# Output projection of seven token tiles as three one-pass products of high and low parts

## The reference

```python
mixed = jnp.concatenate([o_gla, o_gdn], axis=-1).astype(h.dtype)
h = h + mixed @ w_out[i]
h = h + moe_ffn(rmsnorm(h, g_moe[i]), w_router[i], b_router[i], w_gate_up[i], b_gate_up[i],
                w_down[i], b_down[i])
```

## Time and profile before

| | |
|---|---|
| time, three runs | 2509.98 us median (2505.41 to 2510.16) |
| the profiled execution | 2505.38 us, its span 2503.6 us |
| PE busy | 2424.4 us, 97% |
| DVE, ACT busy | 1129.9 us (45%), 581.8 us (23%) |
| route stage | about 648 to 798 us of the span |
| HBM traffic | 210 GB/s over the span |

### The profile page before, as it was taken

The page is one execution under the profiler, slowest core; times in us unless marked ns, Lnnn a source line. Parts: engine busy times, 40 slices in busy tenths (PEclk is TensorE's granted clock), DMA queues, the critical chain, the costliest instruction groups (busy, mean ns, idle before and its releaser), DMA issues. The chain is left out here.

```text
span 2503.6 us, 49492 instructions
## 1 busy us (share of the span) xinstructions
PE 2424.4 (97%) x19869; PEld 2195.0 (88%) x19870; DVE 1129.9 (45%) x1888; ACT 581.8 (23%) x1239; POOL 330.0 (13%) x345
## 2 busy tenths in 40 slices
PE   8999999999898899999999999999999999999898
PEld 6787787688444899999999999999999999999776
DVE  4667618635323523333344344344443434343485
ACT  4434324653112000001110111111111111111265
POOL 0000116252001000000010010010100101010230
PEclk9999997999998999999999999999999999999899
DMA  4111211000621866777788888899898988988562
GB/s 153 43 51 51 89 55 44 26 3 24 245 71 63 277 220 235 249 253 266 272 285 299 290 292 313 311 313 325 310 323 314 320 311 315 317 316 317 194 212 76
DMA packets 113983, 528.52 MB, mean 211 GB/s; under 512 B 15044, under 2 KB 38808, under 8 KB 64696
## 3 DMA queue, kind: packets, MB, share of 16 engines
q1 hardware_dynamic: 99160, 481.16, 54.7%
q0 software_dynamic: 14688, 45.37, 5.6%
HBM read 485.84 MB, written 40.63 MB: 210 GB/s over the span
## 5 line engine op out<-in xcount | busy, mean ns | idle before, releaser
L1886 PE MATMUL ex_psum<-ex_xT,weight_ring_a 128*128 128x134 f32 (+14 forms) x7168 | 900.4, 287 | 4.8 <-DVE ex_xT L1871 4.8
L1886 PEld LDWEIGHTS ex_psum<-ex_xT,weight_ring_a 128*128 128x128 f32 x7168 | 885.9, 192 | 6.3 <-issue 5.6
L1928 PE MATMUL ex_psum<-ex_hT,weight_ring_b 128*128 128x134 f32 (+14 forms) x4096 | 506.0, 286 | 0.0
L1928 PEld LDWEIGHTS ex_psum<-ex_hT,weight_ring_b 128*128 128x128 f32 x4096 | 503.0, 191 | 0.0
L1747 POOL DMA_INDIRECT ex_rows<-xn_dram,ex_list x170 | 164.7, 969 | 1368.2 <-DVE ex_list L1790 1317.4
L1896 DVE TENSOR_SCALAR ex_gate<-ex_psum,bias_gate_up 128x192 f32<-128x192 f32 x256 | 92.8, 404 | 526.4 <-PE ex_psum L1886 525.9
L1900 DVE TENSOR_SCALAR ex_up<-ex_psum,bias_gate_up 128x192 f32<-128x192 f32 x256 | 95.0, 413 | 379.1 <-PE ex_psum L1886 379.1
L1913 ACT ACTIVATE ex_sig<-ex_gate 128x384 f32<-128x384 f32 x128 | 66.9, 523 | 700.9 <-DVE ex_gate L1896 700.5
L1938 ACT ACTIVATE ex_yT<-ex_psum,bias_down 128x192 f32<-128x192 f32 x256 | 83.1, 436 | 564.6 <-PE ex_psum L1928 564.6
L2189 PE MATMUL project_psum<-n_hi,w_in_hi 128*128 128x512 f32 x464 | 187.0, 403 | 2.9 <-DVE n_lo L520 2.9
L2189 PE MATMUL project_psum<-n_lo,w_in_hi 128*128 128x512 f32 x464 | 181.6, 391 | 0.0
(11 more groups left out here) (347 smaller groups left out, 2475.5 us busy)
## 6 DMA issues: line engine op xcount, KB each, us to landing
weight_ring_a<-in_w_gate_up SPq DMA_DIRECT2D x224, 1024.0 KB, 5.5
weight_ring_b<-in_w_down SPq DMA_DIRECT2D x128, 1024.0 KB, 6.9
weight_ring_b<-in_w_gate_up SPq DMA_DIRECT2D x32, 1024.0 KB, 6.3
y_dram<-ex_y SPq DMA_DIRECT2D x80, 192.0 KB, 6.0
w_in_pieces<-in_w_in SPq DMA_DIRECT2D x29, 512.0 KB, 3.6
y_dram<-ex_y SPq DMA_DIRECT2D x52, 128.0 KB, 5.3
project_work<-in_x SPq DMA_DIRECT2D x8, 512.0 KB, 7.1
gates_dram<-project_work POOLq DMA_DIRECT2D x16, 256.0 KB, 2.9
```

Of the source, the lines that this page charges most:

```text
L1886: mm = pe.matmul(self.ps[:, bank, i * CAP:i * CAP + width], w[:, k, i * P:(i + 1) * P], self.xT[:, k, 0:width], start=(k == 0), stop=(k == ...
L1928: mm = pe.matmul(self.ps[:, bank, first:first + width], w[:, i, j], self.hT[:, k, 0:width], start=(k == 0 and j % 2 == 0), stop=(k == KT - ...
```

## The change

Tile 0 is projected as before. For tiles 1 to 7 the projection is done in fp32r: 48 products of 512 columns a tile (high x high, high x low, low x high for each of the 8 pieces and 2 halves).

- The high part of w_out (`w_hi`) stands in slots 3 to 6, the high part of two tiles' mixed values (`mix_hi`) in slot 2, the low part of w_out on w_out itself, and the low part of the mixed values on `g.mixA` and `g.mixB`.
- ACT makes the high parts with copies, DVE the low parts with subtractions. The low part of a piece of w_out waits for tile 0's read of that piece (`w_read`). The parts of tiles 1 and 2 are made at the start, those of tile t+3 in round t of the loops.
- PE waits for the low parts: 2t of them before tile t, and piece by piece for w_out in tile 1.
- SP issues slots 0 and 1 where all seven were, and slots 2 to 6 after the last projection, ahead of slot 7 and of the last store.
- DVE's wait for the norm's gains moves from the start of its work to in front of `norm(0)`, behind the splits.

```diff
+        slot_bytes = 4 * 2 * D
+        w_hi = standing_at("w_out_hi", [P, KT, D], g.ring_a_at + 3 * slot_bytes)
+        w_lo = standing_at("w_out_lo", [P, KT, D], g.ring_b_at + slot_bytes)
+        mix_hi = standing_at("mixed_hi", [P, 2, KT, P], g.ring_a_at + 2 * slot_bytes)
+        mix_lo = [standing_at(f"mixed_lo_{i}", [P, NH, T], at) for i, at in enumerate((g.mixA_at, g.mixB_at))]
...
-            for i in range(7):
+            def first_weights(i):
                 sp.dma_start(ring_slot(g, i).rearrange("p (k n) -> p k n", k=KT), weight_source(g, 0, i)).then_inc(g.w_in_ring[i], 16)
+
+            for i in range(2):
+                first_weights(i)
             for t in range(NT):
...
+            sp.wait_ge(proj, NT)
+            for i in range(2, 7):
+                first_weights(i)
             sp.wait_ge(squared, NT)
...
+                if t >= 1:
+                    pe.wait_ge(mix_lo_done, 2 * t)
                 for k in range(KT):
...
+                    else:
+                        if t == 1:
+                            pe.wait_ge(w_lo_done, k + 1)
+                        hi, lo = mix_hi[:, t % 2, k, :], mix_lo[k // NH][:, k % NH, t * P:(t + 1) * P]
+                        for n, (left, right) in enumerate(((hi, w_hi), (hi, w_lo), (lo, w_hi))):
+                            for half in range(2):
+                                mm = pe.matmul(ps[:, 2 * (t % 2) + half, :], left, right[:, k, half * HALF:(half + 1) * HALF],
+                                               start=(k == 0 and n == 0), stop=(k == KT - 1 and n == 2))
...
+            def split_mixed(t):
+                if t >= 3:
+                    act.wait_ge(proj, t - 1)
+                for i, of in enumerate(mixed_halves):
+                    act.copy(mix_hi[:, t % 2, NH * i:NH * (i + 1), :], of(t)).then_inc(mix_hi_done, 1)
+
+            split_mixed(1)
+            for k in range(KT):
+                if k % 2 == 0:
+                    act.wait_ge(w_out_in[k // 2], 16)
+                act.copy(w_hi[:, k, :], w_out[:, k, :]).then_inc(w_hi_done, 1)
+            split_mixed(2)
             root(0)
             root(1)
             for t in range(NT):
                 keep_turned(t)
+                if t + 3 < NT:
+                    split_mixed(t + 3)
...
-            dve.wait_ge(bc_in, 32)
...
+            split_mixed(1)
+            for k in range(KT):
+                dve.wait_ge(w_hi_done, k + 1)
+                dve.wait_ge(w_read, k + 1)
+                dve.tensor_tensor(w_lo[:, k, :], w_out[:, k, :], w_hi[:, k, :].bitcast(F32), ALU.subtract).then_inc(w_lo_done, 1)
+            split_mixed(2)
+            dve.wait_ge(bc_in, 32)
             norm(0)
...
             for t in range(NT):
+                if t + 3 < NT:
+                    split_mixed(t + 3)
                 if t + 2 < NT:
                     norm(t + 2)
```

More of the change, by code:

```diff
@@ L1385, in route, with standing_at @@
         w_out = g.ring_b[:, 1:5].rearrange("p s n -> p (s n)").rearrange("p (k n) -> p k n", k=KT)
+        def standing_at(name, shape, offset):
+            return nc.alloc_sbuf_tensor_at("rt_" + name, shape, F32R, offset=offset)
+        slot_bytes = 4 * 2 * D
[3 more added lines that the diff above has]
+        mix_lo = [standing_at(f"mixed_lo_{i}", [P, NH, T], at) for i, at in enumerate((g.mixA_at, g.mixB_at))]
         w_router = sb("w_router", [P, KT, E])
@@ L1411, in route @@
         w_out_in = [sem(f"w_out_in{i}") for i in range(KT // 2)]
+        w_hi_done, w_read, w_lo_done = sem("w_out_hi"), sem("w_out_read_by_tile_0"), sem("w_out_lo")
+        mix_hi_done, mix_lo_done = sem("mixed_hi"), sem("mixed_lo")
         w_in_s, bc_in, rows_in = sem("router_in"), sem("broadcasts_in"), sem("bias_rows_in")
@@ L1423, in route, with mixed @@
         block = ph.enter_context(nc.Block())
+        def mixed(k, t):
+            return (g.mixA if k < NH else g.mixB)[:, k % NH, t * P:(t + 1) * P]
+        mixed_halves = [lambda t: g.mixA[:, :, t * P:(t + 1) * P], lambda t: g.mixB[:, :, t * P:(t + 1) * P]]
         @block.sync
@@ L1466, in project_tile @@
                     pe.wait_ge(summed, t - 1)
+                if t >= 1:
+                    pe.wait_ge(mix_lo_done, 2 * t)
                 for k in range(KT):
[L1468 to L1474, removed]
+                    mix = mixed(k, t)
+                    if t == 0:
+                        if k % 2 == 0:
+                            pe.wait_ge(w_out_in[k // 2], 16)
+                        for half in range(2):
+                            mm = pe.matmul(ps[:, half, :], mix, w_out[:, k, half * HALF:(half + 1) * HALF], start=(k == 0), stop=(k == KT - 1))
+                        mm.then_inc(w_read, 1)
+                    else:
[3 more added lines that the diff above has]
+                        for n, (left, right) in enumerate(((hi, w_hi), (hi, w_lo), (lo, w_hi))):
+                            for half in range(2):
+                                mm = pe.matmul(ps[:, 2 * (t % 2) + half, :], left, right[:, k, half * HALF:(half + 1) * HALF],
+                                               start=(k == 0 and n == 0), stop=(k == KT - 1 and n == 2))
+                if t == 0:
+                    pe.wait_ge(w_read, KT).then_inc(proj, 1)
+                else:
+                    mm.then_inc(proj, 1)
             def turn_tile(t):
@@ L1609, in place, with split_mixed @@
                 dve.tensor_scalar(g.place[:, t, 0:E], spot[:], -1.0, None, ALU.add).then_inc(place_done, 1)
+            def split_mixed(t):
+                for i, of in enumerate(mixed_halves):
+                    dve.wait_ge(mix_hi_done, 2 * (t - 1) + i + 1)
+                    dve.tensor_tensor(mix_lo[i][:, :, t * P:(t + 1) * P], of(t), mix_hi[:, t % 2, NH * i:NH * (i + 1), :].bitcast(F32), ALU.subtract).then_inc(mix_lo_done, 1)
             dve.memset(g.place[:, :, E:E + 1], -1.0).then_inc(list_done, 1)
+            split_mixed(1)
[5 more added lines that the diff above has]
+            dve.wait_ge(bc_in, 32)
             norm(0)
@@ L2558, in program @@
                     g.mixA = mixed.enter_context(nc.sbuf_tensor("mixed_gla", [P, NH, T], F32, side="right"))
+                    g.mixA_at = nc.sbuf_top
                     with stage_signals(nc, "gla") as sem:
@@ L2561, in program @@
                 g.mixB = mixed.enter_context(nc.sbuf_tensor("mixed_delta", [P, NH, T], F32, side="right"))
+                g.mixB_at = nc.sbuf_top
                 with stage_signals(nc, "delta") as sem:
@@ L2565, in program @@
             g.ring_a = sb("weight_ring_a", [P, RING_A, 2 * D])
+            g.ring_a_at = nc.sbuf_base - RING_A * 4 * 2 * D
             g.ple_weights = (g.ring_a[:, 0:4].rearrange("p s n -> p (s n)").rearrange("p (k n) -> p k n", k=KT),
@@ L2580, in program @@
             g.ring_b = routed.enter_context(nc.sbuf_tensor("weight_ring_b", [P, 12 - RING_A, 2 * D], F32))
+            g.ring_b_at = nc.sbuf_base - (12 - RING_A) * 4 * 2 * D
             with stage_signals(nc, "route") as sem:
```

## The result

| | before | changed |
|---|---|---|
| time, median of 4 runs | 2508.38 us (2505.41 to 2510.16) | 2493.48 us (2490.33 to 2494.55) |
| ratio, 95% interval | | 0.9938, 0.9924 to 0.9953 |
| span of the profiled execution | 2503.6 us | 2491.8 us |
| mean granted clock over it | | 0.976 |

The changed kernel is faster by 14.9 us, and the forecast of 2493.0 us lies 0.5 us from its median. The trace shows that this closeness is partly luck: two sizes in the sum were too favourable, a gain was missing from it, and the three nearly cancel.

What follows compares the result with a forecast made beforehand. TensorE's projection was taken to bound the routing loop, a chain of small steps its end. Saving 20.1 less tail loss 4.4 gave 15.7 us: 2494.3 from the median 2509.98, stated as 2493, range 2488 to 2502.

Steps and rivals of the forecast that it cites:

- The bound: Routing stage: TensorE's projection sets each round, 13.83 of 16.01 us; behind the last projection, a chain of small steps does.
- the products' saving: Projection of tiles 1 to 7: 48 fp32r products at 0.228 us, 10.96 against 13.83 us a tile, 20.1 us saved.
- rival A: Projection: one-pass products take 0.216 us each, 10.37 us a tile, 19.8 us net gain; chance 0.08 including an unheld store.
- The splits: ACT's copies and DVE's subtractions making high and low parts, beside tile 0 and in the loop: hidden, cost nothing.
- 2.7 us of slack: Before tile 1: w_out's last subtraction done at 669.5, tile 1 starting at 672.20.
- The tail: Stage end: five moved loads hold the last store, landing 19.2 us after the last projection instead of 14.8; 4.4 us lost.
- The bounds of 0 and 6.5: Tail loss in us: 0 if the store were not held, 6.5 if the loads ran slower than the earlier seven.
- The bias rows: Between tile 0 and tile 1: the rows' late landing, with bias turns waiting until 670.62, stays unchanged.
- Clock: TensorE's lower clock level stays in the tail and early expert stage; 2 us allowed either side, 0 in the sum.
- D: Projection loop: new products run at the lower clock, 0.427 us each, up to 51 us slower, 2560; chance 0.05.

## Why the prediction was right, and where it was not

**The bound, and the products' saving.** The mechanism held: each round is shorter by its products' saving and nothing took their place. The term was too large: 20.1 us were put down, with 2.87 a tile. The six rounds give 15.9 and tile 1 2.6, 18.5 in all, 2.64 a tile. The failed step is the transfer of 0.228 us from the earlier trace rows: here a step takes 0.231, which makes 0.15 us a tile, and the first and the last pair of a stream take 0.54 and 0.55 instead of 0.46 (748.23 to 748.77, 758.95 to 759.50), 0.17 more. So the products of a tile take 11.27 us where 10.96 were put down. The rest of a round is 0.08 shorter (2.10 against 2.18 us), which leaves the 0.23 between 2.87 and 2.64. The sum gave this term no bound of its own and needed one, since the step was carried from one stage to another. The kernel with two products has 0.228 in this very stage, so that it was not the stage that made the difference; what did is open.

The Trainium skill, FP8 and Floating Point Precision, section TensorE Precision Notes, with its four passes for true FP32, gives an estimate of 13.83 x 0.75 = 10.4 us for the three one-pass products of a tile. The trace has 11.27, a ratio of 0.81. The measurement decides: for this form and size the estimate promises 0.9 us a tile too much, and rival A, whose 10.37 us a tile is the same figure, is out.

**The splits.** Right. The last subtraction of w_out is done at 668.5, and tile 1 starts at 669.47. The timeline of DVE in the changed kernel shows the chain: released piece by piece by tile 0, then the low part of tile 2's values, then the norm's sum of tile 0.

```profile
667.27 1.23 DVE L1671 TENSOR_TENSOR rt_w_out_lo<-weight_ring_b,rt_w_out_hi 128x1024 fp32r<-128x1024 f32 x1 [0.49 <-PE rt_psum L1498]
668.42 0.68 DVE L1664 TENSOR_TENSOR rt_mixed_lo<-mixed_gla,rt_mixed_hi 128x512 fp32r<-128x512 f32 x1
...
669.62 1.22 DVE L1624 TENSOR_TENSOR h<-rt_psum,rt_x 128x1024 f32<-128x1024 f32 x1
...
706.12 1.23 DVE L1624 TENSOR_TENSOR h<-rt_psum,rt_x 128x1024 f32<-128x1024 f32 x1 [6.23 <-PE rt_psum L1506]
```

The forecast had 669.5 for the subtractions on the clock of the trace of before, whose tile 0 stands 1.05 us later: the same point. Its 2.7 us of slack were only 1.0, because tile 1 came 1.7 us earlier than it thought.

**The tail.** The mechanism held, the store behind the loads, and both ways of freeing it took the loss away. The size was 4.4 us and is 6.3. The store was to land 19.2 us behind the last projection and landed after 20.9 (780.4 - 759.5). It repeats: 20.5 to 21.7 us in the six traces with the store last. The weights ran at 423 GB/s at first, and the last megabyte slower: of the six, the fifth landed at 775.2, 15.7 us behind the last projection where the forecast's steps give 15.3, and slot 7 at 778.7, 3.5 us later where 2.55 were put down, and the store 1.6 later where 1.4 were. The other 0.2 us is the barrier: 1.2 us from the landing to the next stage's first instruction, where it had been 0.9 behind the last small step (797.25 to 798.18). The bounds of 0 and 6.5 held the loss. The rows of the loads in the changed kernel:

```profile
762.00:774.00 12.00, 6.07 (x73) 4.49 (x73) 7.20 (x34) 6.59 (x25) 0.00 (x0) 0.57 1.01 423
...
776.00:778.00 2.00, 0.00 (x0) 0.00 (x0) 0.00 (x0) 0.00 (x0) 0.00 (x0) 0.50 0.88 338
```

The Trainium skill, DMA: Bandwidth & Descriptors, section Where 436 GB/s comes from, puts the limit for transfers from HBM at about 358 GB/s. While the queue was full the rows show 423, so that the page's limit did not bind here; the loss that the forecast missed lies in the end of the burst, where the rate fell to 338, and not in the rate before it. The end of a burst is not slow everywhere: with the store issued earlier, first or fourth, the last load landed 2.5 us behind the one before it in three traces (777.35 and 779.83 in the second trace of the store fourth) and 3.9 in one. Why it was slow here isn't shown.

**The bias rows.** This step failed in its reasoning: "which I leave as it is: they are issued ahead of the weights". The loads behind the rows in the queue did matter. With seven large ones behind them the last rows landed 8.7 and 8.3 us after their issue, and TensorE had stood for 2.40 and 2.02 us; with two behind them they landed after 7.0 to 7.4, and it had stood for 0.5 to 0.95, in every kernel of that kind. Of the 1.7 us between the waits of the first two profiles only 0.8 lie on the path (22.93 and 22.16 us from the stage's start to tile 1), since the first w_out pieces landed 0.9 us later. That too goes with the loads: these pieces land 4.9 to 5.0 us after their issue in the three traces with seven loads in front, 5.8 to 6.0 in the ten others; by what means isn't shown. On top comes tile 1's stretch at the lower clock level, 1.7 us, which is absent in all kernels with the short wait. That the wait brings the stretch is shown by the rows moved ahead; by what means seven loads delay rows that are queued ahead of them is not shown.

**Clock.** No fall inside the loop, as expected; D is out. In the tail the clock stands at 0.50 and rises in the next stage, at places that differ from execution to execution. That may be the source of the experts' 1566 to 1570 us, but no run isolated it.

**The sum again.** Forecast 20.1 - 4.4 = 15.7. Measured in the route stage 18.5 - 6.3 + 0.8 + 1.7 = 14.7. Two terms were too favourable by 3.5 us in all (1.6 and 1.9), and a gain of 2.5 was not foreseen. That the time came within 0.5 us is luck in part: the sum gave 2494.3 from the first median of before, and 2493 was chosen between two levels.

## What to carry to other kernels

When loads are moved behind the last work of a stage, ask what small transfer in the same queue the barrier waits for, and put that one at the place in the queue where it lands just ahead of the computing chain's end: last it cost 6 us here, while first or fourth of seven both took them back. A wait before a long stream of products costs more than its length if the clock falls in it: 2.0 to 2.4 us of waiting cost 3.3 to 3.9. A price per product taken from another stage wants a margin of some 3% (11.27 us a tile against 10.96), since over many products it adds up to a tenth of the gain.

## What the hardware showed that was not expected

- The last of two loads of small rows landed 8.3 to 8.7 us after its issue with seven 1 MB loads directly behind it in the queue, and 7.0 to 7.4 with two. The first pieces of w_out, at the head of the same queue, did the opposite: 4.9 to 5.0 us with seven, 5.8 to 6.0 with two.
- Two small DVE casts that started beside two POOL MEMSETs ended with the first MEMSET (1.39 us) in nearly all traces and with the second (2.70 us) in one, on which the next stage's gathers were late by 1.3 us. Loads at 423 GB/s beside them made no difference.
- The last of six 1 MB loads, with a store behind it, took 3.5 us beyond the one before it, with the rate at 338 GB/s where it had been 423; with the store issued earlier it took 2.5 in three traces of four.
- A one-pass product of 512 columns steps at 0.231 us here, whether one PSUM bank takes the products or two take turns, and at 0.228 in the first stage; without the third of the three products it steps at 0.228 here too.
